# Hybrid decoder layer: search flags in PSUM, four banks for the pooled units, last tile's sums on GpSimd, the window mean's scaling on ScalarE, another order of the seven gate products

## The reference, cut to what matters

```python
(u_a, z_a, q, k, v, z_b, q_idx, k_idx, w_idx, g_a, g_b) = split(h @ w_in)
y_a = multiscale_pool(u_a, w_group, scale) * silu(z_a)     # windows 2, 4, 8, 16: mean over the window minus u_a, then 128x128 per group
attn = dsa_sparse_attention(q, k, v, q_idx, k_idx, w_idx)  # top 256 keys of each query by relu(q_idx . k_idx) . w_idx, then attention
y_b = attn * silu(z_b)
merged = sigmoid(g_a) * (y_a @ w_branch_a) + sigmoid(g_b) * (y_b @ w_branch_b)
x = x + gate * (merged @ w_out)
```

## Time and profile before

| | |
|---|---|
| median of three runs | 830.41 us (828.32 to 831.02) |
| profiled execution | 828.4 us, its span 826.3 us |
| granted clock of TensorE, mean | 0.985 |
| busy, share of the span | PE 95%, DVE 72%, ACT 58%, POOL 51% |

### The profile page before, as it was taken

The page is one execution under the profiler, slowest core; times in us unless marked ns, Lnnn a source line. Parts: engine busy times, 40 slices in busy tenths (PEclk is TensorE's granted clock), DMA queues, the critical chain, the costliest instruction groups (busy, mean ns, idle before and its releaser), DMA issues.

```text
span 826.3 us, 13063 instructions
## 1 busy us (share of the span) xinstructions
PE 785.1 (95%) x4318; PEld 663.3 (80%) x4323; DVE 595.3 (72%) x1199; ACT 475.5 (58%) x890; POOL 421.7 (51%) x383
## 2 busy tenths in 40 slices
PE   7999999999998799979999987999999999999998
PEld 5988988887886588658888865788888888888987
DVE  5876687797999888578878887456667895772422
ACT  5764456662457576569998534488777884330100
POOL 1102623044589498976877635666888821540000
PEclk9999999999999899999999998999999999999999
DMA  9930210023342112443343343743432203754331
GB/s 348 391 104 1 67 37 27 1 64 121 116 159 90 38 57 103 147 140 104 114 141 103 102 140 117 245 149 135 134 115 90 65 23 132 255 166 134 123 107 58
DMA packets 65649, 98.43 MB, mean 119 GB/s; under 512 B 6153, under 2 KB 37165, under 8 KB 65582
## 3 DMA queue, kind: packets, MB, share of 16 engines
q1 hardware_dynamic: 55970, 78.70, 29.7%
q10 hardware_dynamic: 7692, 12.60, 4.1%
q0 software_dynamic: 1920, 6.29, 1.9%
HBM read 71.36 MB, written 26.21 MB: 118 GB/s over the span
## 4 chain that ended last, share of the span: by engine, by line
PE 71%; DVE 15%; ACT 4%; DVEq 3%; issue 3%; POOL 2%; POOLq 1%; ACTq 0%
PE pp L883 13%; PE pp L885 13%; PE pp L884 13%; PE pp L1374 3%; PE pt L1346 3%; PE ps L1124 3%; PE ps L1123 3%; PE ps L883 3%; PE ps L885 3%; PE ps L884 3%; DVE score L2494 2%; DVE junk L2519 1%; POOL w_lo L2090 1%; PE pp L919 1%; PE pt L942 1%
## 5 line engine op out<-in xcount | busy, mean ns | idle before, releaser
L1647 ACT ACTIVATE ps<-score,cand 128x896 f32<-128x896 f32 (+3 forms) x96 | 96.6, 1006 | 24.2 <-DVE cand L2538 16.8
L883 PE MATMUL pp<-hT_hi,w_hi 128*128 128x512 f32 x192 | 76.8, 400 | 11.1 <-ACT ua L1677 9.3
L2717 DVE TENSOR_TENSOR pT<-pt,pT 128x512 fp32r<-128x512 f32 (+3 forms) x96 | 50.5, 554 | 45.2 <-ACT pT L1912 41.7
L885 PE MATMUL pp<-hT_hi,w_lo 128*128 128x512 f32 x192 | 76.3, 398 | 0.0
L884 PE MATMUL pp<-hT_lo,w_hi 128*128 128x512 f32 x192 | 76.2, 397 | 0.0
L883 PE MATMUL pp<-w_hi,hT_hi 128*128 128x256 f32 (+1 forms) x208 | 69.0, 332 | 1.8 <-POOL w_lo L823 1.1
L2519 DVE TENSOR_SCALAR_CACHE_REDUCE junk<-score,cand 128x384 uint8<-128x384 f32 (+3 forms) x94 | 68.2, 752 | 3.2
L884 PE MATMUL pp<-w_lo,hT_hi 128*128 128x256 f32 (+1 forms) x208 | 67.5, 324 | 0.0
L885 PE MATMUL pp<-w_hi,hT_lo 128*128 128x256 f32 (+1 forms) x208 | 67.4, 324 | 0.0
L823 POOL TENSOR_TENSOR w_lo<-w_raw,w_hi 128x1024 fp32r<-128x1024 f32 x23 | 59.7, 2611 | 14.9 <-ACT w_hi L818 13.7
L818 ACT ACTIVATE w_hi<-w_raw 128x1024 fp32r<-128x1024 f32 x36 | 36.8, 1054 | 42.0 <-PE pp L885 40.9
(11 more groups left out here) (398 smaller groups left out, 2411.6 us busy)
## 6 DMA issues: line engine op xcount, KB each, us to landing
w_raw<-in_w_in SPq DMA_DIRECT2D x36, 512.0 KB, 3.7
sgb_spill<-stage SPq DMA_DIRECT2D x16, 256.0 KB, 2.0
sga_spill<-stage SPq DMA_DIRECT2D x16, 256.0 KB, 2.1
stage<-sga_spill SPq DMA_DIRECT2D x16, 256.0 KB, 3.5
ma_spill<-stage POOLq DMA_DIRECT2D x16, 256.0 KB, 2.6
gate_w<-in_w_ada SPq DMA_DIRECT2D x16, 256.0 KB, 2.7
w_raw<-in_w_out SPq DMA_DIRECT2D x8, 512.0 KB, 4.5
e_in<-sgb_spill SPq DMA_DIRECT2D x16, 256.0 KB, 3.0
```

What stands on the lines that cost most here:

```text
L883: nc.tensor.matmul(o, a_hi, b_hi, start=first, stop=False)
L885: return nc.tensor.matmul(o, a_lo, b_hi, start=False, stop=last)
L1647: done = nc.scalar.activation(ps[1][:, 0:keys(b)], score[:, score_at(b):score_at(b + 1)], ACT.Sign, scale=-1.0, bias=cand[:, n:n + 1].bitc ...
L2717: v.tensor_tensor(pT[:, j // 2 % 2, t0:t1, 1, j % 2, :], pt[n % 2][:, 0:(t1 - t0) * P].rearrange("p (t q) -> p t q", q=P), pT[:, j // 2 % ...
```

## The change

1. **Flags.** `accept` is no longer an SBUF tensor but the first six columns of the PSUM bank pt0, in `narrow` and in `search_take`.
2. **Banks.** The eight ua units use four banks (pp0, pp1, the halves of ps0), the z units two as before. The wait for the last index score's read of ps0 moves ahead of the ua units; the first group product waits for the copy of the last ua unit.
3. **Sums of tile 3** go from VectorE (after round 3) to GpSimd (after the first window); `sums_out(3)` waits for GpSimd.
4. **Window mean.** The scaling by 1/w goes from GpSimd to ScalarE (`window_scale`), with two new semaphores; `window_mean` becomes `window_sum` and `window_rest`, and GpSimd's order around them changes.
5. **Order of products.** The product of the activations' last half (j = 5) moves to j = 3, the two products with reloaded sums to 4 and 5; outputs 21 and 22 change places, `weight_sums` makes its third and fourth sum earlier, `middle(c, 3)` is gone and its addition is done in `middle(c, 4)`, which then frees both banks.
6. **Reloads.** The loads of sums 6 to 9 no longer wait for sum_low(5), those of 10 and 11 wait for two lows less; all six count on one semaphore.
7. **Search rounds.** 14 and 15 stand before the gate chunks now, 16 to 30 in chunks 1 to 5, none in chunks 0 and 6. ScalarE's order between rounds, copies and splits changes; `block_hi(0..3)` goes ahead of `sum_high(0..2)`, behind round 14.

```diff
-    pp_bank = [n % 2 for n in range(PP_HT - NG * PRODUCTS)]
+    pp_bank = [n % 2 for n in range(PP_HT - NG * PRODUCTS - 16)]
+    pp_bank += [n % 4 for n in range(8)] + [n % 2 for n in range(8)]
...
+        accept = pt[0][:, 0:NSEL].bitcast(I32)
...
+        def pp_home(n):
+
+            b = pp_bank[n]
+            return pp[b] if b < 2 else ps[0][:, (b - 2) * HALF:(b - 1) * HALF]
...
             sp.wait_ge(mix_full, 2 * GROUPS)
-            sp.wait_ge(s_lo, 4 + 6)
             for l in range(6, 10):
                 load_sum(l)
             for l in range(10, 12):
-                sp.wait_ge(s_lo, 4 + l - 1)
+                sp.wait_ge(s_lo, 4 + l - 3)
                 load_sum(l)
...
-        G_SEARCH = {(0, 4): 14, (6, 0): 30}
+        G_SEARCH = {}
         for n in range(15):
-            G_SEARCH[1 + n // 3, 2 * (n % 3)] = 15 + n
+            G_SEARCH[1 + n // 3, 2 * (n % 3)] = 16 + n
...
+            pe.wait_ge(ps_free_a, ps_done[ps_at[("idx", NT - 1, H - 1)]][0])
             for i in range(2):
                 channel_chunk("ua", i)
             pe.wait_ge(wg_lo_done, 1)
-            pe.wait_ge(ps_free_a, ps_done[ps_at[("idx", NT - 1, H - 1)]][0])
...
                 if j == 3:
+                    return hT_hi[:, 4 + k, last], hT_lo[:, 4 + k, last]
+                if j == 4:
                     return s3[:, 0, k, :], s3[:, 1, k, :]
-                if j == 4:
+                if j == 5:
                     return s1[:, 0, k, :], s1[:, 1, k, :]
-                if j == 5:
-                    return hT_hi[:, 4 + k, last], hT_lo[:, 4 + k, last]
...
+            def window_scale(g):
+
+                w, side = 2 << g, g % 2
+                act.wait_ge(win_summed, g + 1)
+                nc.scalar.activation(win[:, 1 - side, w:L], win[:, side, w:L], ACT.Copy, scale=1.0 / w).then_inc(win_scaled, 1)
```

GpSimd, VectorE:

```diff
             sums(2)
-            window_mean(0)
+            window_sum(0)
+            window_rest(0)
+            sums(3)
+            pooled_low(0)
+            window_sum(1)
             split_chunk_lo(pool, name_of[("za", 0)])
-            pooled_low(0)
-            window_mean(1)
+            window_rest(1)
             pooled_low(1)
-            window_mean(2)
+            window_sum(2)
             split_chunk_lo(pool, name_of[("za", 1)])
+            window_rest(2)
             pooled_low(2)
-            window_mean(3)
+            window_sum(3)
+            window_rest(3)
             pooled_low(3)
...
-                if j == 3:
+                if j == 4:
                     dve.drain()
-                    v.tensor_tensor(three, o, two, ALU.add).then_inc(pp_free_v, 1)
-                    return
-                if j == 4:
+                    v.tensor_tensor(three, o, two, ALU.add)
+                    dve.drain()
+                    o = g_bank(c, 3)
+                if j == 5:
                     v.tensor_tensor(two, o, two, ALU.add)
                     dve.drain()
...
-            search(3)
-            sums(3)
-            search(4)
+            for k in range(3, 6):
+                search(k)
             sum_2_low(3)
...
-            search(13)
-            for l in range(4):
+            search(14)
+            for l in range(3):
                 sum_low(l)
+            search(15)
+            sum_low(3)
             branch_y(6)
             branch_y(7)
```

More of the change, by code:

```diff
@@ L732, in _ @@
                 store_gated(chunk, "11")
-                store_gated(chunk, "22")
+                store_gated(chunk, "21")
                 if chunk < NG - 1:
@@ L1226, in gate_product @@
                 n = pp_at[("g", c, j)]
-                if pp_prev[n] is not None:
-                    wait_done(pe, pp_done[pp_prev[n]], pp_free_a, pp_free_v)
-                else:
+                wait_done(pe, pp_done[pp_prev[n]], pp_free_a, pp_free_v)
+                if c == 0 and pp_bank[n] >= 2:
                     pe.wait_ge(ya_done, 2 * GROUPS)
@@ L1786, in _ @@
             ya_store(5)
+            za_unit(6)
+            counts(14)
+            for q in range(4):
+                block_hi(q)
             for l in range(3):
                 sum_high(l)
-            za_unit(6)
-            for q in range(4):
-                block_hi(q)
+            za_unit(7)
+            counts(15)
             sum_high(3)
-            za_unit(7)
             sum_high(4)
@@ L2647, in middle @@
                     dve.drain()
-                v.tensor_tensor(stage[:, n % G_STAGE, :], o, first if j == 2 else two if j == 6 else three, ALU.add).then_inc(pp_free_v, 1)
+                v.tensor_tensor(stage[:, n % G_STAGE, :], o, first if j == 2 else two if j == 6 else three, ALU.add).then_inc(pp_free_v, 2 if j == 4 else 1)
             dve.wait_ge(q_spilled, 16 * NT)
@@ L2657, in _ @@
             sum_2_low(2)
-            search(3)
-            sums(3)
-            search(4)
+            for k in range(3, 6):
+                search(k)
             sum_2_low(3)
-            for k in range(5, 9):
+            for k in range(6, 9):
                 search(k)
@@ L2769, in _ @@
                     mask_begin(5)
-                middle(c, 3)
                 if c == 0:
```

124 lines of the change are left out of this document (65 added, 59 removed).

## The result

The changed kernel takes 839.64 us (median of 4, 838.40 to 840.25) against 830.39 for the one before (4 runs, 828.32 to 831.02): ratio 1.0114, 95% interval 1.0093 to 1.0135, slower by 9 us. The forecast was 829.4, the range 824.5 to 834. The profiled execution took 838.4 us, its span is 836.2 at a mean granted clock of 0.973.

The account below looks back on a forecast made before the run. TensorE, busy 785.1 of 826.3 us, was taken to bound the kernel. -0.2 to chunk 1 and -0.8 at the end make 827.4 of the profiled 828.4; with 2.0 to the median, 829.4 us, range 824.5 to 834.

Parts of the forecast that it names:

- The z units: With four banks and moved work, z units start at 277.6 instead of 281.54: gain 3.9, 7.2 idle in one piece.
- A: Stretch from first pooled unit to first z unit: forecast 50.9 us, 54.9 in the kernel before.
- From there to the first gate product: Last pooled copy near 318.7, then 11.8 on ScalarE: first gate product at 332.2 instead of 334.28.
- B: Stretch from first z unit to first gate product: forecast 54.6 us, 52.7 in the kernel before.
- The first chunk: Gate chunk 0: seventh product at 355.3 against 355.41 before; the reorder shortens waits, 1.0 at most, hidden.
- C: Stretch from first gate product to seventh product of chunk 0: forecast 23.1 us, 21.1 in the kernel before.
- Chunk 1: Second gate chunk begins at 361.8 instead of 361.0, round 14's 0.8 goes two products later: sum to there -0.2.
- D: Stretch from chunk 0's seventh product to chunk 1's third: forecast 11.9 us, 12.0 in the kernel before.
- The last chunks: Chunks 6 and 7: VectorE 0.9 and 0.9 earlier, a new 1.7 wait before chunk 7; taken as -0.8.
- The flags: Search flags in PSUM: waits gone, about 0.45 on each of L2532 and L2538, 29 us of VectorE's busy time.
- rival (c): Flags in PSUM save nothing and the candidate's masking stays 1.1: +1.7, 831.1 us; chance 0.08.
- Rival (b): Two rounds before the gates cost; z units at 280.6 move everything behind by 3: 832.9 us; chance 0.15.

Follow-up runs that it names:

- the second execution: The changed kernel run and profiled once more, word for word: 840.24 us, one run.
- e_round7: Changed kernel with search round 7 moved ahead of ScalarE's copy of pooled unit 6: ratio 1.0088 to the kernel before.
- e_block3: Changed kernel with the split of block 3 moved behind the last z unit's copy: ratio 1.0097 to the kernel before.
- e_order_back: Changed kernel with the gate chunks' products back in the order of the kernel before: ratio 1.0046 to the kernel before.
- e_rounds_back: Changed kernel with search rounds 14, 15 and 30 put back in the gate chunks: ratio 1.0059 to the kernel before.
- f_flags: Kernel before with the search flags in a PSUM bank and nothing else: ratio 0.9960 to the kernel before.
- f_order_round7: Changed kernel without its product order, with search round 7 ahead of pooled unit 6's copy: ratio 0.9994 to the kernel before.
- f_order_rounds_round7: Changed kernel without product order, round 7 ahead of pooled unit 6's copy, rounds 14, 15, 30 back in gate chunks: 823.34 us, ratio 0.9929, the fastest.

## Why the prediction was wrong, step by step

**The z units: right.** Forecast -3.9 in A, measured -3.9 (-2.7 in the second execution), with 7.3 us idle where 7.2 was written, the sums' end and the splits' end each within 0.2 after taking off the later start. The moved sums cost 10.6 (257.16 to 267.8), the lower of the two prices.

**From there to the first gate product: the step that failed.** "Nobody needs those banks before the first group product near 291, so this wait is free" asked who waits for ScalarE by way of PSUM banks alone. It did not ask what the next instructions in ScalarE's queue wait for themselves. Pooled unit 6's copy needs a free `ua` buffer, which GpSimd gives free only behind the moved sums and the weight splits, and the chain to the last pooled copy, which by the forecast "starts near 318.7", runs through what is queued behind that copy. The wait of 4.14 was in no sum; the term missing in B was +3.3 (e_round7). The rest of that step, round 14 in front of the split at 3.6 and the stores' wait, was right: 3.7 measured.

**The first chunk: failed.** Forecast +2.0, measured +5.8 in C. I let the reorder only "shorten waits". Yet the diff shows block 3's wait go from the first weight sum to the third, behind the low parts of blocks 0 and 1: 2.9 (e_block3, e_order_back). Round 15 was in the sum, and e_rounds_back shows 1.6 for it in C. The forecast's +2.0 and these 2.9 leave 0.9 of the 5.8 without a cause shown.

**Chunk 1: failed in size.** "-0.2" was the sum to there; D alone is +3.2 (+2.4 in the second execution), and taking the order back gives 2.8. The clock has a part in it: over the 42 us from each first gate product on, as length, busy PE, granted clock, DMA share, GB/s, before and after:

```profile
334.00:376.00 42.00, 36.11 (x146) 0.96 0.43 142
```

```profile
338.00:380.00 42.00, 32.59 (x107) 0.81 0.44 138
```

Chunk 1's first product ran wholly at the low clock, as its own stretch shows:

```profile
372.00:377.30 5.30, 5.29 (x13) 0.50 0.39 97
```

That is 5.3 us for a product that takes 2.7 at full clock, behind six waits between 333 and 372. The forecast had charged slow clock once, after the longest gap.

**The last chunks: right in kind, low in size.** -0.8 forecast, -2.8 and -1.2 in two executions; the new wait before chunk 7 was forecast at 1.7 and is 2.15. The masking of the candidate, 1.10 before, took 0.16 as forecast (0.2).

**The flags: right.** The waits are gone, and rival (c), that they save nothing, falls by f_flags, where VectorE is busy 566.2 us instead of 595.3: 29.1 less, 29 forecast. The Trainium skill, "SBUF — State Buffer", section "SBUF: two separate sides", has a rule by which these instructions stop contending with GpSimd. This trace agrees with it: 165 and 224 ns at all 31 places. The forecast's estimate from the Trainium skill, "VectorE: DVE Perf Modes", on the TRN2 errata, of 65 ns more for each PSUM source, is not borne out: L2565 takes 224 ns with a PSUM source where L2538 took 224 at its least without one.

**Rival (b)** had the right side and named the rounds, with the wrong trigger ("It decides from a z start behind about 278.5": A was on time, and the moved sums cost their lower price) and about half of the price (2.9). Its 1.2 more of slow clock after the longer gap no run shows: about 13 slow matmuls followed the 7.30, about 12 the 5.85 before. The rounds cost whenever they stand there: 0.65% (f_order_round7 against f_order_rounds_round7).

One way to divide the 1.1% is a ladder of versions, each one step from the next, in microseconds of 830.4: the fastest version is -5.9 against the kernel before; the two rounds ahead of the gates add 5.4 (f_order_round7); the copy of unit 6 ahead of round 7 adds 4.3 (e_order_back); the product order adds 5.6 (the kernel after). The steps meet the measured 9.5 because each starts where the last one ended, so their sum proves nothing; each step by itself is a measurement. In another order the shares differ: the copy of unit 6, worth 4.3 here, is worth 2.2 with the product order in place (e_round7), and there it is not clear of the interval. On this ladder the change holds 6 us of gain and 15 of losses; of the losses the forecast had 3.8 in B and C and 1.7 before chunk 7. What the earlier reloads of the sums do was not tried by itself; they are in the 6.

## What to carry to other kernels

When a producer's work is moved back in its queue, list every consumer that waits for it, and for each what stands queued behind that consumer: a copy that waits for a buffer to be read is such a consumer, and here it was late by 4.1 us and 3.3 of them reached the first gate product. Reordering products reorders their inputs' makers and their buffers' release; both must be walked through at the place where the slowest helper is latest, not on average. Where a change has parts with opposite signs, test it part by part: four of its parts gained here (flags; banks, once the sums had moved; moved sums and moved scaling, each beside the rest) and three changes of order lost more (the two search rounds, the copy of unit 6 ahead of round 7, the products of a chunk).

## What the runs showed of the hardware that I had not expected

- Short waits that follow each other cost as much slow clock as a long one. In the kernel after 13 matmuls start 0.42 us or more apart (1.2 GHz; 0.23 is 2.4 GHz) behind the one wait of 7.30, 13 behind the one of 4.91, six behind the one of 4.54, and 13 again behind four waits of 1.38, 1.93, 0.71 and 0.58 us, 4.6 together (363.8 to 372.0), which had three to six matmuls between them. Over the 42 us from 338 on the granted clock was 0.81.
- A VectorE instruction on six numbers a partition costs 224 ns whether its source is in SBUF or PSUM. With SBUF sources alone it took up to 2.32 us beside GpSimd's work, where it ended with GpSimd's instruction.
- The first 226 us, the same instructions in all kernels, end at 226.7 to 226.9, 227.6, 228.3 to 229.0 or 230.8 to 230.9 in 20 executions, also for one and the same kernel (228.6 and 229.0), and on either side of the change, so single profiles are compared stretch by stretch.
